# A hybrid decoder step on one core: cached attention with its keys and values in four column groups of 32 instead of one

## What is computed

```python
k_past = cache_k[j][page_table].reshape(db, past_len, KV_HEADS, HEAD_DIM)   # 8 x 2048 x 4 x 128
v_past = cache_v[j][page_table].reshape(db, past_len, KV_HEADS, HEAD_DIM)
# 8 query heads, 2 per key head; blocks of 256 keys; per head the 3 blocks with the largest
# q . mean(k), and the new token itself, take part in the softmax
logits = jnp.einsum('bqhd,bqhsjd->bqhsj', qi, kg) * scale
p = jax.nn.softmax(jnp.where(mask, logits, -jnp.inf).reshape(b, qc, ATT_HEADS, -1), axis=-1)
out = jnp.einsum('bqhsj,bqhsjd->bqhd', p.reshape(...), vg)
```

## Time and profile before

| | |
|---|---|
| median of 3 runs | 2118.62 us (2118.04 to 2120.09) |
| profiled execution | span 2117.8 us, 0.8 us below the median of the runs; the page gives no other time for it |
| PE busy | 2014.8 us, 95% |
| DVE, ACT busy | 62%, 44% |
| DMA | 512.34 MB, mean 242 GB/s |
| key matmuls | first starts at 713.23 us |
| value matmuls | first starts at 856.41 us |
| output projection | starts at 972.50 us |

### The profile page before, as it was taken

One profiled execution on the slowest core, in us unless ns is written; L12 is line 12 of the kernel. 1 busy time (PEld: TensorE's weight loads), 2 busy tenths in 40 slices (PEclk: granted clock), 3 DMA queues, 4 the chain that ended last, 5 costly groups with the idle time before them and its releaser, 6 DMA issues.

```text
span 2117.8 us, 27204 instructions
## 1 busy us (share of the span) xinstructions
PE 2014.8 (95%) x10121; PEld 1571.7 (74%) x10121; DVE 1323.2 (62%) x1367; ACT 941.4 (44%) x824; POOL 76.7 (4%) x94
## 2 busy tenths in 40 slices
PE   6998989899999998999799999999999999999997
PEld 4888965899996532325688888888888888888885
DVE  5854863555433211011488797887978889797884
ACT  3541000444320110000277676766767677676772
POOL 1231111000000000000000000000000000000000
PEclk8997987999999999899699999999999999999998
DMA  6231005355548678563199898998989989898990
GB/s 265 99 101 66 1 1 206 142 179 180 182 157 260 211 246 301 188 230 119 60 358 361 321 342 327 351 363 311 342 324 348 357 317 350 320 344 333 339 353 23
DMA packets 96731, 512.34 MB, mean 242 GB/s; under 512 B 10769, under 2 KB 10898, under 8 KB 44418
## 3 DMA queue, kind: packets, MB, share of 16 engines
q1 hardware_dynamic: 81936, 478.50, 60.9%
q10 hardware_dynamic: 13970, 25.46, 3.7%
q0 software_dynamic: 736, 7.21, 1.0%
HBM read 503.91 MB, written 7.21 MB: 241 GB/s over the span
## 4 chain that ended last, share of the span: by engine, by line
issue 67%; PE 27%; DVE 4%; ACT 1%; DMA 0%; SPq 0%; POOLq 0%; POOL 0%; ACTq 0%; DVEq 0%
PE bank L485 5%; PE bank L486 5%; PE bank L487 5%; PE bank L784 3%; PE bank L718 1%; PE bank L696 1%; PE bank L597 1%; PE bank L641 1%; PE bank L621 1%; PE bank L634 1%; DVE w_lo L1381 1%; PE bank L479 1%; ACT w_hi L1040 1%; DVE scr L1437 0%; PE bank L506 0%
## 5 line engine op out<-in xcount | busy, mean ns | idle before, releaser
L1750 DVE TENSOR_TENSOR w_lo<-raw_w,w_hi 128x2048 fp32r<-128x2048 f32 x336 | 768.8, 2290 | 140.8 <-ACT w_hi L1206 137.6
L1206 ACT ACTIVATE w_hi<-raw_w 128x2048 fp32r<-128x2048 f32 x336 | 644.9, 1920 | 429.0 <-PE bank L948 280.1
L946 PE MATMUL bank<-w_hi,xe_hi 128*128 128x512 f32 x896 | 365.6, 408 | 1.5 <-DVE xe_lo L1808 1.5
L948 PE MATMUL bank<-w_hi,xe_lo 128*128 128x512 f32 x896 | 350.8, 392 | 0.0
L947 PE MATMUL bank<-w_lo,xe_hi 128*128 128x512 f32 x896 | 350.2, 391 | 0.0
L486 PE MATMUL bank<-fh_lo,w_hi 128*128 128x264 f32 x704 | 201.8, 287 | 0.0
L946 PEld LDWEIGHTS bank<-w_hi,xe_hi 128*128 128x128 f32 x896 | 169.0, 189 | 36.0 <-issue 1.8
L948 PEld LDWEIGHTS bank<-w_hi,xe_lo 128*128 128x128 f32 x896 | 168.8, 188 | 36.1
L947 PEld LDWEIGHTS bank<-w_lo,xe_hi 128*128 128x128 f32 x896 | 169.2, 189 | 33.7
L946 PE MATMUL bank<-w_hi,aT_hi 128*128 128x512 f32 x448 | 177.1, 395 | 0.0
L947 PE MATMUL bank<-w_lo,aT_hi 128*128 128x512 f32 x448 | 174.6, 390 | 0.0
(11 more groups left out here) (329 smaller groups left out, 2500.9 us busy)
## 6 DMA issues: line engine op xcount, KB each, us to landing
raw_w<-in_moe SPq DMA_DIRECT2D x336, 1024.0 KB, 4.8
raw_w<-in_ffn_w SPq DMA_DIRECT2D x42, 1024.0 KB, 4.8
ring<-in_k_pages SPq DMA_DIRECT2D x96, 256.0 KB, 3.1
raw_w<-in_gdn_in SPq DMA_DIRECT2D x16, 1024.0 KB, 6.9
ring<-in_v_pages SPq DMA_DIRECT2D x64, 256.0 KB, 4.7
ring<-in_v_pages ACTq DMA_DIRECT2D x64, 256.0 KB, 4.1
ring<-in_att_in SPq DMA_DIRECT2D x4, 2048.0 KB, 7.9
ring<-in_k_pages ACTq DMA_DIRECT2D x32, 256.0 KB, 3.7
```

What stands on the lines that cost most here:

```text
L946: mm(out, hi, move_hi, start=first, stop=False)
L948: return mm(out, lo, move_hi, start=False, stop=last)
L1206: A(w_hi[:, p % SPLIT, :], raw_w[:, p % RAW, :], ACT.Copy).then_inc(split_hi, 1)
L1750: V.tensor_tensor(w_lo[:, p % SPLIT, :], raw_w[:, p % RAW, :], w_hi[:, p % SPLIT, :].bitcast(F32), ALU.subtract).then_inc(split_lo, 1)
```

## The change

The score rows move from 64 to 128 partitions: key head k writes to the partitions 32k to 32k+31, where row 2b+r is sequence b's head 2k+r (16 of 32 rows hold scores, the others zeros). A key head's stationary tile is now 128x32, and its matmuls write into its own column group of 32. The loop over heads becomes the inner one. The values' stationary tile becomes 32 columns of `prob_T` (four sequences at a time), and page j of every four writes to the partitions 32j to 32j+31, so that the four groups hold sums over different pages. DVE copies the whole bank to `o_parts`, and `turn_o` adds the four groups and picks a head's rows by four matmuls with two columns of `mod32`, a sum of the identity's four blocks. The softmax runs on 128 rows.

```diff
-        prob = scr[0:64, at:at + N_PAGES * PAGE]; at += N_PAGES * PAGE
+        prob = scr[:, at:at + N_PAGES * PAGE]; at += N_PAGES * PAGE
...
-        q_wide = hflat[:, 0:NS * KVH * 64].rearrange("p (i r) -> p i r", r=64)
+        q_wide = hflat[:, 0:NS * KVH * 32].rearrange("p (i r) -> p i r", r=32)
...
-        o8 = carve(scr, at - 1536, NS, DK)[0:8]
-        o_wide = carve(scr, at - 512, KVH, DK)[0:8]
+        o_parts = carve(scr, at - 1536, 2, KVH * DK)
...
-                for h in range(KVH):
-                    for q in range(2):
-                        last = mm(bank[2 * (c % 2) + q][0:64, :].rearrange("p (g t) -> p g t", t=PAGE),
+                for q in range(2):
+                    for h in range(KVH):
+                        last = mm(bank[2 * (c % 2) + q][32 * h:32 * h + 32, :].rearrange("p (g t) -> p g t", t=PAGE),
                                   q_wide[:, KVH * b + h, :], keys[:, q, :, h, :],
-                                  start=(b == 0 and h == 0), stop=(b == NS - 1 and h == KVH - 1), skip_group_check=True)
+                                  start=(b == 0), stop=(b == NS - 1), skip_group_check=True)
...
             def turn_o(b):
                 pe.wait_ge(o8_done, b + 1)
-                nc.tensor.transpose(bank[6][:, H * b:H * (b + 1)], o8[:, b, :], ident[0:8, 0:8]).then_inc(o8_turned, 1)
+                for k in range(KVH):
+                    col = 8 * (b % 4) + 2 * k
+                    last = mm(bank[6][:, H * b + 2 * k:H * b + 2 * k + 2], o_parts[:, b % 2, DK * k:DK * (k + 1)],
+                              mod32[:, col:col + 2], start=True, stop=True)
+                last.then_inc(o8_turned, 1)
...
                 for g in range(PPC):
-                    page = (c % 2) * PPC + g
-                    last = mm(bank[b % 4][0:8, :], prob_T[:, page, H * b:H * (b + 1)],
-                              ring[:, n % SLOTS, 512 * g:512 * (g + 1)], start=(page == 0), stop=(page == N_PAGES - 1))
+                    page, j = (c % 2) * PPC + g, g % 4
+                    last = mm(bank[b % 4][32 * j:32 * j + 32, :], prob_T[:, page, 32 * (b // 4):32 * (b // 4) + 32],
+                              ring[:, n % SLOTS, 512 * g:512 * (g + 1)], start=(page < 4), stop=(page >= N_PAGES - 4),
+                              skip_group_check=True)
...
                     link(V.memset(hflat, 0.0))
+                    V.tensor_reduce(mod32, ident.rearrange("p (k m) -> p m k", m=32), AX, ALU.add)
...
-                if b >= 1:
-                    dve.wait_ge(o8_done, b)
-                link(V.tensor_tensor(o_wide, bank[b % 4][0:8, :].rearrange("p (k d) -> p k d", k=KVH),
-                                     kv_of_head.unsqueeze(2).to_broadcast([8, KVH, DK]), ALU.mult))
-                V.tensor_reduce(o8[:, b, :], o_wide.rearrange("p k d -> p d k"), AX, ALU.add).then_inc(o8_done, 1)
+                if b >= 2:
+                    dve.wait_ge(o8_turned, b - 1)
+                V.tensor_copy(o_parts[:, b % 2, :], bank[b % 4]).then_inc(o8_done, 1)
```

More of the change, by code:

```diff
@@ L266, in program @@
         hflat = hT[:, :, :].rearrange("p k t -> p (k t)")
-        q_wide = hflat[:, 0:NS * KVH * 64].rearrange("p (i r) -> p i r", r=64)
-        q_own = hflat.rearrange("p (b k r) -> p b k r", b=NS, k=KVH)[:, :, :, 0:2]
-        prodn = hflat[:, NS * KVH * 64:NS * KVH * 64 + 64]
+        q_wide = hflat[:, 0:NS * KVH * 32].rearrange("p (i r) -> p i r", r=32)
+        q_own = hflat[:, 0:NS * 130].rearrange("p (b x) -> p b x", x=130)[:, :, 0:P]\
+            .rearrange("p b (k m) -> p b k m", m=32)[:, :, :, 0:2]
+        prodn = hflat[:, NS * 130:NS * 130 + P]
+        prod_own = prodn.rearrange("p (k m) -> p k m", m=32)[:, :, 0:2 * NS].rearrange("p k (b r) -> p k r b", r=2)
         prob_T = hflat[:, 0:N_PAGES * 64].rearrange("p (g r) -> p g r", r=64)
@@ L278, in stat @@
             return v
[L280 to L283, removed]
+        st_max, st_sum, pen, biases, sums = (stat(P, BLOCKS) for _ in range(5))
+        cmp_b, eq_b = stat(P, BLOCKS, BLOCKS), stat(P, BLOCKS, BLOCKS)
+        m_neg, l_new, p_new, r_den = (stat(P, 1) for _ in range(4))
+        rd_diag, p_diag = stat(P, NS * H), stat(P, NS * H)
+        mod32 = stat(P, 32)
+        own_row = ident.rearrange("p (k m) -> p k m", m=32)[:, :, 0:2 * NS].rearrange("p k (b r) -> p b k r", r=2)
         o_new = stat(P, NS, H)
-        kv_of_head = stat(8, KVH)
         assert st[0] <= 48 * T - at
-        o8 = carve(scr, at - 1536, NS, DK)[0:8]
-        o_wide = carve(scr, at - 512, KVH, DK)[0:8]
+        o_parts = carve(scr, at - 1536, 2, KVH * DK)
         rl = sm(3, NE)
@@ L854, in _ @@
                     pe.wait_ge(pT_sb, H)
-                    mm(bank[6][0:64, 0:1], prodn, ones[:, 0:1], start=True, stop=True).then_inc(lnew_ps, 1)
+                    mm(bank[6][:, 0:1], prodn, ones[:, 0:1], start=True, stop=True).then_inc(lnew_ps, 1)
             pe.wait_ge(diag_done, 1)
@@ L864, in _ @@
                     last.then_inc(probT_ps, 1)
-            mm(bank[7][:, 0:64], ones[0:64, :], p_diag, start=True, stop=True).then_inc(probT_ps, 1)
+            mm(bank[7][:, 0:64], ones, p_diag, start=True, stop=True).then_inc(probT_ps, 1)
             def turn_o(b):
                 pe.wait_ge(o8_done, b + 1)
-                nc.tensor.transpose(bank[6][:, H * b:H * (b + 1)], o8[:, b, :], ident[0:8, 0:8]).then_inc(o8_turned, 1)
+                for k in range(KVH):
[3 more added lines that the diff above has]
+                last.then_inc(o8_turned, 1)
             for c in range(2 * NS):
@@ L1191, in _ @@
             for n in range(BLOCKS):
-                A(prob[:, 256 * n:256 * (n + 1)], bank[n // 2][0:64, 256 * (n % 2):256 * (n % 2 + 1)], ACT.Exp,
+                A(prob[:, 256 * n:256 * (n + 1)], bank[n // 2][:, 256 * (n % 2):256 * (n % 2 + 1)], ACT.Exp,
                   bias=biases[:, n:n + 1], scale=SCALE, accum_out=sums[:, n:n + 1])
@@ L1701, in _ @@
             dve.wait_ge(lnew_ps, 1)
-            V.tensor_copy(l_new, bank[6][0:64, 0:1])
-            V.tensor_reduce(kv_of_head, ident[0:8, 0:8].rearrange("p (k r) -> p k r", r=2), AX, ALU.add)
+            V.tensor_copy(l_new, bank[6][:, 0:1])
             for q in range(4):
                 dve.wait_ge(k_read, 2 * NS - 1 + q // 2)
-                t = bank[q][0:64, :].rearrange("p (n t) -> p n t", n=2)
+                t = bank[q].rearrange("p (n t) -> p n t", n=2)
                 V.tensor_reduce(st_max[:, 2 * q:2 * q + 2], t, AX, ALU.max)
@@ L1709, in _ @@
             link(ins)
-            other, own = st_sum.unsqueeze(1).to_broadcast([64, 8, 8]), st_sum.unsqueeze(2).to_broadcast([64, 8, 8])
+            other, own = st_sum.unsqueeze(1).to_broadcast([P, 8, 8]), st_sum.unsqueeze(2).to_broadcast([P, 8, 8])
             V.tensor_tensor(cmp_b, other, own, ALU.is_gt)
             link(V.tensor_tensor(eq_b, other, own, ALU.is_equal))
-            link(V.tensor_tensor(eq_b, eq_b, before[0:64], ALU.mult))
+            link(V.tensor_tensor(eq_b, eq_b, before, ALU.mult))
             link(V.tensor_tensor(cmp_b, cmp_b, eq_b, ALU.add))
@@ L1726, in _ @@
             link(V.reciprocal(r_den, r_den))
-            link(V.tensor_scalar(rd_diag, ident[0:64, 0:64], r_den, None, ALU.mult))
+            link(V.tensor_scalar(rd_diag.rearrange("p (b k r) -> p b k r", b=NS, r=2), own_row, r_den, None, ALU.mult))
             V.tensor_scalar(p_diag, rd_diag, p_new, None, ALU.mult).then_inc(diag_done, 1)
```

2 lines of the change are left out of this document (1 added, 1 removed).

## The result

The changed kernel takes 2013.23 us (median of 4 runs, 2011.86 to 2018.05); the kernel before took 2119.13 us beside it. The ratio is 0.9498, with an interval of 0.9482 to 0.9513. The forecast was 2026 us, so the gain was right in sign and mechanism and 13 us too small.

The account below looks back on a forecast made before the run. PE's passes bound the cache stage; made faster, it would be bound by transfers. The output projection starts at 879 instead of 972.5 us (-93.5), plus 1 us of clock: -92.5 from 2118.6 gives 2026 us, range 2009 to 2100.

Parts of the forecast that it names:

- The expected signs: Cache stage: key passes under 0.43 us apart, chunks 1.8 to 3.5 us, engines at 0.9 or more, projection near 879 us.
- The matmuls: Key and value matmuls on PE: same number and columns, neighbours on four column groups overlap; a chunk falls from 7.0 to 3.4 us.
- the middle case: Key and value chunks: passes start in order, one matmul per 0.43 us, 3.4 us a chunk, between 7.0 and 1.75.
- The rate of the transfers: From key chunk 7's landing at 724 us: 25 x 2.10 MB at 339 GB/s, 6.19 us each, 155 us, ending at 879.
- the low end of my range: Cache stage loads at 377 GB/s: 139 us of loads, -109 us, total 2009 us.
- The softmax block of 17.7 us is carried over: Between keys and values: the softmax keeps its 17.7 us on 128 rows, so values start at 800.4 us.
- So the queue never runs dry: Value loads: eight chunks keep engines busy to 823 us; the ninth needs value chunk 0 read, at 804.
- The clock: First part of the output projection: PE's clock can fall in waits, costing 0 to 8 us, 1 taken.
- this rival: Cache stage: clock falls and takes the overlap back, or overlap under two; 5.2 us a chunk, 2079 us, chance 0.10.
- The turnings: Between value chunks on PE: each turning becomes 8 passes, 0.88 us instead of 0.15; seven among the values.
- Nothing overlaps: Rival, key and value passes: they keep 0.43 us, the dearer turnings show, 2123.7 us; chance 0.08.
- Emptying at each change of group: Rival, 256 key and value matmuls: each group change empties the array, 0.05 to 0.16 us each, 2137 to 2165 us; chance 0.08.

Follow-up runs that it names:

- the pairs: Against the changed kernel, neighbouring key and value matmuls come in pairs on the same column group; 2013.5 us, ratio 0.9505.
- two groups: Against the changed kernel, keys and values write only two of the four column groups, sums not the reference's; 2024.97 us, ratio 0.9556.
- one group: Against the changed kernel, all key and value matmuls write to rows 0 to 31, same tile sizes and count; 2124.98 us, ratio 1.0023.

## Why the prediction was right, and 13 us short

The expected signs came, but for one: starts under 0.43 us apart, a chunk between 1.8 and 3.5 us, PE released by DMA of `ring`, prompt steps of 5.31 us (5.04 forecast), and an end set by the transfers. The DMA engines were full but for the hole at 800 to 820 us (0.77), where 0.9 and more was forecast. By its steps:

**The matmuls.** I took two matmuls beside each other, 3.4 us a chunk. It is four, 1.92 us, and the reason for the middle case (passes start in order) fell with the pairs. That the choice hardly mattered, since both lie under a chunk's load, held only roughly: two groups, at 3.5 us a chunk, cost 12 us, in the values.

**The rate of the transfers** is the term that was mis-sized, and most of the 13 us. I took 339 GB/s, 6.19 us a chunk. Measured, a full queue moves 387 GB/s, 5.42 us, over 63 us on end (737 to 800). From the landing of key chunk 7 (725.1) to the projection's first weights (867.0) it took 141.9 us and not 155: 25 x (5.42 - 6.19) = -19.3, +1.0 for a slower start up to 812.9, +6.0 for the hole and the refilling behind it (812.9 to 829.7), -0.7 in the rest. The 339 of the experts went with a share of 0.90: a row of engines that weren't full. The sum scaled another row to a full share, 362 / 0.96 = 377, which gives 863 us for the projection; that was the low end of my range, and the better choice. That it lies within 4 us of the 867.0 is partly luck: 377 is still below 387, and the hole is not in it. The Trainium skill, "DMA: Bandwidth & Descriptors", "Measured", has 341 GB/s for a single transfer of 1 MB, issued from GpSimd, and 425 for one of 16 MB; the 387 of this stream of 256 KB pages from SP and ACT lies between them.

**"The softmax block of 17.7 us is carried over"** was wrong: it took 38.1. The cover that I left out was ACT's own queue. Before, PE read the keys so late that ACT had its pages issued when it was wanted; now the keys are done at 771.7, and ACT still has 25 us of pages ahead of the exponentials. It cost little only because the transfers set the end: with the exponentials first the values start 15.5 us earlier and the stage is 3.0 us shorter. Two errors also offset each other here: the keys were read 11 us earlier than forecast (771.7, 782.7), so that the values started 9 us late (809.8, 800.4) and not 20.

**"So the queue never runs dry"** failed with it. Value chunk 7 had landed at 812.9, while value chunk 0 was read only after its start at 809.8: the next page landed at 817.1.

**The clock.** I took 1 us. It is 0.50 while PE idles from 780 to 800 us, the 1.2 GHz level, and 0.68 at 840 to 860. Of the six waits for a value page, the three of 1.7 to 3.7 us were followed by chunks of 3.3 to 3.6 us instead of 1.92, the three of 0.8 to 0.9 us were not. By the Trainium skill's section "HAM oscillation" ("TensorE: Matmul & The Clock Gate"), which the prediction named, a wait for DMA between bursts of matmuls sends the clock back; here the rows agree for the longer waits and not for the short ones. A chunk at the lower level still lies inside the 5.4 us of its transfer, so that this rival had its mechanism and not its price. The projection's first 48 rows took 12.40 us, and 12.61 before: my microsecond was double counting, since before had that loss too. At full clock it would be 10.92, as with two groups.

**The turnings** (0.98 us from start to next start, 0.88 forecast) and DVE's copy (0.69) were as said, and hidden. Behind the projection's start nothing changed (-105.5 of -105.8).

**The other rivals.** Nothing overlaps: shown false by the change, and what it would have cost shown by one group (2125). Emptying at each change of group: neighbouring groups start 0.01 us apart, so there is no such price.

## What to carry to other kernels

Where a float32 matmul has 32 output columns or fewer, putting neighbours on four column groups made sixteen 512-column passes take 1.9 us instead of 7.0, in both orders of the groups that were tried; what it is worth is then read from the next bound, here the transfers at their rate for a full queue, not at an average of a stage that is bound otherwise. When one stage becomes several times faster, ask of every engine that serves it whether it is also issuing transfers: its arithmetic stands behind them. And load started earlier, or issued on a second queue beside large transfers, may land later where the ring is full or the shares are unequal.

## What the runs showed of the hardware that was not expected

- Passes of other column groups start past a waiting one: 1.95 us a chunk with pairs on the same group, 1.92 with groups in turn, and 14 ns instead of 7 between neighbouring starts.
- Half a page by partitions (64 of 128) takes 0.63 us, hardly less than the whole page's 0.68, at a share of 1.08 and 207 GB/s; half a page by row length takes 0.39. A share near 1 doesn't tell that the bytes are at their limit.
- One engine's issue of pages slows once its pages take about 14 us to land: in the change ACT issues one every 1.08 us from 760.7 to 782.2 and every 1.29 us from there to 796.4 (1.05 to 1.07 throughout where pages of half rows landed after 3 us), and the engine's arithmetic waits behind them.
- The last three pages of ACT's queue took 21 to 27 us to land beside SP's 2 MB loads, and 11 to 13 us where those came after them.
